# One half of a shift vector summed straight into columns by one-column matmuls, at the opening of a hybrid RG-LRU / gating / conv-FFN block

## What is computed

```
mod = silu(c) @ w_ada + b_ada
shift1, scale1, gate1, shift2, scale2, gate2 = split(mod, 6)
h = rmsnorm(x, g) * (1 + scale1) + shift1
z = h @ w_in
```

## Time and profile before

| | us |
|---|---|
| median of 3 runs | 1523.43 |
| lowest, highest | 1523.28, 1523.55 |
| the profiled execution | 1523.99 |
| its span | 1522.2 |

### The profile page before, as it was taken

One profiled execution on the slowest core, in us unless ns is written; L12 is line 12 of the kernel. 1 busy time (PEld: TensorE's weight loads), 2 busy tenths in 40 slices (PEclk: granted clock), 3 DMA queues, 4 the chain that ended last, 5 costly groups with the idle time before them and its releaser, 6 DMA issues.

```text
span 1522.2 us, 19720 instructions
## 1 busy us (share of the span) xinstructions
PE 1500.3 (99%) x6772; PEld 1233.7 (81%) x6772; DVE 1249.3 (82%) x1577; ACT 821.6 (54%) x1222; POOL 410.7 (27%) x307
## 2 busy tenths in 40 slices
PE   7999999999999999999999999999999999999998
PEld 4788888878888888888887788888888888888887
DVE  6997888777777786688859999999999987777775
ACT  5378988734544473422535555555555553444447
POOL 0024334522223223000100433333333321333324
PEclk9999999999999999999999999999999999999999
DMA  9531233374443364473421244444444436777722
GB/s 348 185 105 55 77 91 92 112 251 138 153 144 123 108 214 145 156 241 102 167 62 42 62 149 164 155 156 152 153 152 152 153 112 231 250 249 249 249 66 112
DMA packets 212227, 231.12 MB, mean 152 GB/s; under 512 B 9920, under 2 KB 164896, under 8 KB 211360
## 3 DMA queue, kind: packets, MB, share of 16 engines
q1 hardware_dynamic: 212128, 229.86, 45.7%
HBM read 167.95 MB, written 61.87 MB: 151 GB/s over the span
## 4 chain that ended last, share of the span: by engine, by line
PE 91%; DVE 6%; issue 1%; DMA 1%; ACT 1%; SPq 0%; DVEq 0%; ACTq 0%
PE ps L886 74%; PE ps L964 4%; PE ps L985 2%; PE ps L1154 1%; PE ps L1250 1%; PE ps L1097 1%; PE ps L1232 1%; PE ps L1014 1%; DVE wop L1901 1%; PE ps L1058 1%; DVE hidw L2588 1%; DMA xtok<-in_x 1%; DVE hq L2531 1%; DVE n L2523 0%; PE ps L1051 0%
## 5 line engine op out<-in xcount | busy, mean ns | idle before, releaser
L1313 ACT ACTIVATE wop<-raw 128x512 fp32r<-128x512 f32 (+1 forms) x541 | 307.1, 571 | 363.2 <-PE ps L886 235.0
L1901 DVE TENSOR_TENSOR wop<-raw,wop 128x512 fp32r<-128x512 f32 (+1 forms) x541 | 372.5, 692 | 120.8 <-ACT wop L1313 119.5
L727 POOL TENSOR_TENSOR raw<-raw,raw 128x512 f32<-128x512 f32 (+1 forms) x69 | 99.4, 1440 | 879.6 <-DVE wop L1901 427.7
L886 PE MATMUL ps<-hq,wop 128*128 128x512 f32 x888 | 214.2, 391 | 1.3 <-DVE wop L1901 0.9
L886 PEld LDWEIGHTS ps<-hq,wop 128*128 128x128 f32 x888 | 166.1, 188 | 38.3 <-DVE hq L2531 1.6
L886 PE MATMUL ps<-dq,wop 128*128 128x512 f32 x840 | 190.6, 389 | 0.0
L886 PE MATMUL ps<-yq,wop 128*128 128x512 f32 x792 | 190.4, 389 | 0.0
L886 PEld LDWEIGHTS ps<-dq,wop 128*128 128x128 f32 x840 | 157.7, 188 | 32.7
L886 PEld LDWEIGHTS ps<-yq,wop 128*128 128x128 f32 x792 | 148.5, 188 | 31.1 <-DVE wop L1901 0.2
L1915 DVE TENSOR_TENSOR ps<-ps,snap_p 128x512 f32<-128x512 f32 x136 | 94.5, 695 | 53.4 <-PE ps L886 52.8
L1328 ACT ACTIVATE snap_p<-ps 128x512 f32<-128x512 f32 x136 | 81.2, 597 | 101.7 <-PE ps L886 101.5
(11 more groups left out here) (288 smaller groups left out, 2584.7 us busy)
## 6 DMA issues: line engine op xcount, KB each, us to landing
dq<-hid_keep SPq DMA_DIRECT2D x35, 1024.0 KB, 7.1
raw<-in_w_in SPq DMA_DIRECT2D x96, 256.0 KB, 4.2
raw<-in_w_up SPq DMA_DIRECT2D x96, 256.0 KB, 3.3
hid_keep<-part_b SPq DMA_DIRECT2D x40, 512.0 KB, 3.0
hid_keep<-part_t SPq DMA_DIRECT2D x20, 512.0 KB, 3.1
raw<-in_w_down SPq DMA_DIRECT2D x80, 128.0 KB, 2.3
ada_w<-in_w_ada SPq DMA_DIRECT2D x8, 1024.0 KB, 11.4
gate_keep<-tg SPq DMA_DIRECT2D x16, 512.0 KB, 4.7
```

Of the source, the lines that this page charges most:

```text
L727: nc.gpsimd.tensor_tensor(s1, a21, a22, ALU.add).then_inc(s_made, 1)
L886: done = nc.tensor.matmul(bank, left[:, w, lk, :], right[:, x, rk, :], start=(first and w == 0 and x == 0), stop=(last and w == 1), skip_g ...
L1313: nc.scalar.activation(wop[n % 4][:, 0, 0:depth[n], :], raw[slot][:, 0:depth[n], :], ACT.Copy).then_inc(f_hi, 1)
L1901: V.tensor_tensor(wop[n % 4][:, 1, 0:kd, :], raw[slot_of[n][0]][:, 0:kd, :], wop[n % 4][:, 0, 0:kd, :].bitcast(F32), ALU.subtract).then_in ...
```

## The change

Part 1 (first half of the shift) no longer goes through a row. PE multiplies the row tiles 4 and 5 of `w_ada` as stationary operand by one column of `cact`, eight products of one column, into four columns of `ps[2]`. DVE's accumulator, which now also holds row tile 3, is summed by `part_columns(1)`. DVE adds bias and the two sums in two steps. ACT's second `row_copy`, PE's `add_row(1)` and `row_to_columns(1)` go. In DVE's list two `log_terms` move behind `normed(5)`, `mod_columns(1)` moves ahead of `lo(0)`, and `norm_low(0)` ahead of `lo(1)` and `normed(1)`.

```diff
-        PE_ROWS = ((0, 1, 2, 4), (3, 4, 5), (), ())
+        PE_ROWS = ((0, 1, 2, 4), (4, 5), (), ())
...
+            def direct_columns(p, ks):
+                pe.wait_ge(ada_landed[p][ks[0] // KH], 16)
+                for j in range(KH):
+                    for k in ks:
+                        nc.tensor.matmul(ps[2][:, 1, j:j + 1], ada_w[p][:, k, j * P:(j + 1) * P], cact[:, k:k + 1],
+                                         start=(k == ks[0]), stop=(k == ks[-1]))
...
             add_row(0)
-            modulation_rows(1, PE_ROWS[1][:1])
             pe.wait_ge(param_col, len(ROWS))
             row_to_columns(0)
-            modulation_rows(1, PE_ROWS[1][1:])
-            add_row(1)
+            pe.wait_ge(xT_copied[1], COPIER.count(1))
+            direct_columns(1, PE_ROWS[1])
             pe.wait_ge(s1_ready, 1)
-            row_to_columns(1)
+            part_columns(1)
...
-            row_copy(0)
+            row_copy()
             hi(0)
-            row_copy(1)
             hi(1)
...
                 c0 = (KT if p in SCALE_PARTS else 0) + p // 2 * KH
+                if p == 1:
+                    step(V.tensor_tensor(mod[:, c0:c0 + KH], ps[2][:, 1, 0:KH], C("b_ada", c0, KH), ALU.add))
+                    return V.tensor_tensor(mod[:, c0:c0 + KH], mod[:, c0:c0 + KH], ps[3][:, 1, KH * p:KH * p + KH], ALU.add)
...
-            mod_pieces(1, (0, 1, 2))
-            log_terms(7, 6)
+            mod_pieces(1, (0, 1, 2, 3))
             scale_columns(0)
             mod_pieces(1, (6, 7))
             normed(0)
+            mod_columns(1).then_inc(shift_ready, 1)
             lo(0)
+            norm_low(0)
+            lo(1)
             normed(1)
-            mod_columns(1).then_inc(shift_ready, 1)
-            lo(1)
-            norm_low(0)
             lo(2)
...
-            log_terms(5, 4, 3, 2)
+            log_terms(7, 6, 5, 4, 3, 2)
```

More of the change, by code:

```diff
@@ L815, in column_sums @@
                 return last
-            ROW_IN = (ps[3], ps[2])
+            ROW_IN = (ps[3],)
             COLS = ps[3][:, 1, :]
@@ L1361, in _, with row_copy @@
                 param_copy(t)
[L1363 to L1367, removed]
+            def row_copy():
+                act.wait_ge(row_sum, 1)
+                nc.scalar.activation(mod_row[0:1, :], ps[3][0:1, 0, :], ACT.Copy).then_inc(row_ready, 1)
             def norm_high(k):
```

## The result

The changed kernel takes 1526.2 us at the median of 18 runs (1524.87 to 1527.29); the kernel before, on the same chips, 1523.6 us (1523.14 to 1524.19, 18 runs). The ratio is 1.0016, 95% interval 1.001 to 1.0022. That is 2.6 us slower, where + 0.7 was forecast, and outside the range (up to 1525.6). The 18 times lie in two groups: nine from 1524.87 to 1525.68 (middle one 1525.18, + 1.6 over before), nine from 1526.72 to 1527.29 (middle one 1527.04, + 3.4). The median lies in the gap between them, so + 2.6 is the time of no execution. The profiled execution (1525.68) is the slowest of the lower group.

What follows compares the result with a forecast made beforehand. It took the start of lo(7) on DVE to set when PE's unbroken work begins: + 0.91 (second wait, addition) - 0.70 (DVE idle) + 0.80 (log terms) - 0.28 (idle) = + 0.73 us, 1524.2 us; range 1522.6 to 1525.6.

Steps and rivals of the forecast that it cites:

- The place: End of the opening: PE's unbroken work starts behind lo(7) on DVE, at 64.75 us before, near 65.5 after.
- The scale came no earlier: Part 0: row_to_columns(0) still needs ACT's copy, so it starts at 26.10 against 26.12 us.
- the added piece cost nothing: DVE's added piece, 0.77 us from 26.23, stays hidden since DVE waits for PE until 27.27.
- the direct products: The shift's eight one-column products on PE: 1.90 us, from 27.17 to 29.07; twice that as upper bound.
- both waits for ACT: DVE waits 0.70 us ahead of norm_low(0) and, newly, 0.70 ahead of norm_low(1).
- The log terms: Four instructions, 0.80 us, ahead of lo(7), less 0.28 of DVE idle there; 0.53 in the rivals' sums.
- With a slow `keep_busy` the gates start near 33.9: PE's gate products after the shift: 33.9 us with a slow keep_busy, 33.2 with a fast one, before 34.83.
- rival (B): Clock falls during PE's one-column products, taking up to twice the time: + 3.3 us, 1526.8; chance 0.05.
- The load formula of the Trainium skill: Weight load takes stationary columns divided by 1.2 GHz at any clock: 16 loads 1.7 us, no extra cost.
- - 0.70 (DVE's idle at 50.50): Term of the sum: DVE's idle of 0.70 us before the second scale is taken out, offsetting DVE's lateness.
- DVE goes on 0.21 us later: At the second scale DVE gets there at 50.71 instead of 50.50; the work behind shifts by 0.21.
- PE's lead ... ends at the second scale: PE's 60 products end near 47.5 to 48 instead of 49.5; then PE waits for DVE's part 2 accumulator.

Runs made afterwards that it cites:

- logs_cover: Changed kernel with the two moved log terms between lo(0) and norm_low(0), in DVE's wait for ACT; median 1526.17 us, ratio 1.0015.
- gap512: Changed kernel plus one unread 512-column product in PE's wait ahead of the scale's columns; median 1525.62 us, ratio 1.0013.
- logs_late_before: Kernel before with only the two log terms moved behind normed(5); median 1524.15 us against 1523.64, ratio 1.0003.
- gap_wide: Changed kernel plus an unread 512-column product ahead of the scale's columns, and the shift's products 128 columns wide; median 1525.99 us, ratio 1.0017.
- wide: Changed kernel with the shift's twelve products each of 128 moving columns instead of one; median 1525.97 us, ratio 1.0016.
- gap_wide_hold: gap_wide plus one unread 512-column product ahead of the columns of part 2 and of part 3; median 1525.49 us, ratio 1.0012.
- the cures taken together on best_plain: best_plain plus a 512-column product ahead of the scale's columns and 128-column products for the shift; median 1523.55 us, ratio 1.0001.
- best_plain: Changed kernel, DVE reordered: shift's addition behind lo(0), normed(1) ahead of norm_low(0), one log pair ahead of norm_low(4); median 1525.25 us, ratio 1.0008.
- keep512: Changed kernel plus one unread 512-column product between the scale's columns and the direct products; median 1526.87 us, ratio 1.0024.
- rows45: Kernel before, row path kept, PE multiplying only row tiles 4 and 5 for the shift, log terms late; median 1524.49 us, ratio 1.0008.
- mid_wide: Changed kernel with 128-column products, normed(1) ahead of norm_low(0), shift behind lo(0), log terms ahead of scale_columns(2); median 1524.5 us, ratio 1.0004.

## Why the prediction was wrong

**Right.** The place: PE's unbroken work starts behind `lo(7)`, and the chain through DVE sets it. In all 16 profiles of this study the time of the execution less the start of `lo(7)` lies between 1458.5 and 1459.6 us. The scale came no earlier; the added piece cost nothing; the direct products took 1.95 us where the clock was up (1.90 in the sum); both waits for ACT are there at 0.61 and 0.62; DVE has no idle time left at the second scale or ahead of `lo(7)`. The log terms: 0.53 in the sum, 0.51 measured alone.

**Wrong: the step on the clock.** "With a slow `keep_busy` the gates start near 33.9" priced the early fall at nothing. I had written that it "may fall here too, rather earlier", let it slow only `keep_busy`, and given the slow one-column products 0.05 as rival (B). They were slow in both profiles of the changed kernel: `part_columns` alone in one (+ 0.48 more than with the clock up, by the shifts 3.72 and 3.25), direct products too in the other (+ 1.89, by 5.14 and 3.25). The same differences appear at `lo(7)`: 1.42 - 0.94 = 0.48 and 2.83 - 0.94 = 1.89. (Where one-column products ran with the clock up, in logs_cover and gap512, the shift stands 3.13 and 3.15 behind the bias; against these the slow products cost 0.1 more.) The argument against (B) had also counted badly: the new list leaves PE waiting not once but three times there, 0.77, 0.31 and 0.45 us. (B)'s mechanism was right and belonged in the forecast. Its price of + 3.3 is near the upper group's + 3.4, in part by luck: it had the shift 2.6 us late, where it was 2.0 to 2.1, and it took out the 0.70 of the next paragraph. The load formula of the Trainium skill that was weighed against (B) ("TensorE: Matmul & The Clock Gate", "LDWEIGHTS (loading the stationary operand)") names no level of the clock; that it holds at both was the prediction's reading. By that reading the products would not have slowed down; at the lower level 16 instructions of them took 3.57 us, 0.22 each, against 0.12 at the upper. The measurement decides: they slow down by 1.8.

**Wrong: the term "- 0.70 (DVE's idle at 50.50)".** The sum took this idle for a part of the old order. It is there in the profiled execution of before, whose clock fell at 33.5 and whose 60 products took 14.85 us; in logs_late_before, with the same order and the clock up, they took 13.91 and there is no such idle. So with the clock up on both sides nothing pays for DVE's lateness: the second scale is 1.10 us late (0.70 second wait, 0.20 second addition, 0.20 the shift), where "DVE goes on 0.21 us later" was forecast, and with the log terms `lo(7)` is 1.6 late, not 0.73. That + 0.94 came so near to + 0.73 holds only against the one execution in which the sum was made.

**Unpriced: PE's later wait.** "PE's lead ... ends at the second scale" was read as free. In five variants in which the shift came early the clock falls once more behind that wait: at 0.50 from 49.9 to 53.1 in gap_wide and from 50.4 to 53.6 in wide, for instance, and 24 products take 7.3 instead of 5.7 us. In these profiles `lo(7)` stands 15.3 us behind the second scale instead of 14.8 (logs_cover, which moves the log terms, aside). Neither profile of the changed kernel has this fall (24 products in 5.71 and 5.75 us): it explains why holding the clock early did not help much by itself, and is not shown as a part of the changed kernel's time. Filling the wait took 0.5 us off the median (gap_wide 1525.99, gap_wide_hold 1525.49).

**Missed: one profile is one moment of the clock.** All terms came from one execution, in which the clock was up until 33.5. Its falls come at other times in other executions. In the old order an execution without that fall wins time in the 60 products and so at `lo(7)`. In the changed order PE's speed in these products is worth nothing: in all seven profiles with the changed list and late log terms the second scale stands 20.4 us behind the shift, while the 60 products take from 14.13 to 15.29 us.

So the changed kernel's time is made of this, counted from an old-order execution with its clock up: 0.5 log terms; 1.1 the second wait, the second addition and the later shift; and 0.5 or 1.9 the slow one-column products. Together + 2.1 and + 3.5; against the profiled execution of before, whose clock fell, it is + 1.4 and + 2.8. The two groups stand at + 1.6 and + 3.4 over a median of before in which executions of both kinds can be mixed; in what shares, no run shows. That the slow products are what costs is shown in the two profiles and borne out by gap512, in which no run is in the upper group, and by the cures taken together on best_plain (1.1 to 1.7). What keep512's slowest runs were stays open, as does what the missing product (rows45) and the one-column products contribute to the early fall.

## What to carry to other kernels

When a stretch of 512-column products next to a wait gives way to one-column ones, price everything behind it at the lower clock as well: here they took 3.57 us instead of 1.95. A matmul of one column is nearly as long as one of 128 (1.95 and 2.05 us for 16 instructions), so wider ones cost little to try; whether they alone hold the clock is not shown, and in mid_wide they did not. Before an idle stretch is taken out of a sum, ask whether another execution of the same kernel has it too. An instruction is free only in the place where another wait covers it; two pairs of tiny ones moved out of such a place cost half a microsecond. Where the times fall into groups, take a profile from each before summing anything.

## What the runs showed of the hardware that was not expected

The same program has its clock changes at different moments from execution to execution: in the changed kernel the granted clock is down from 29.9 us in one profile and from 27.3 us in the other. At the lower level (granted clock 0.50, 1.2 GHz) one-column products with 128 x 128 weights take 0.22 us an instruction, at the upper 0.12; 128-column ones at the upper 0.13. The 32 transposes at the very start took between 5.13 us (gap_wide) and 6.61 (keep512), and the scale's bias came the later the longer they took, broadly, from 27.07 to 28.49; every profile shows a granted clock of 1.00 there, so that it is the clock is a guess.
